# Two attentions of a fused model step: one DVE pass for mask and row maximum, and a product of two tensors on GpSimd

## The reference, cut to what matters

```python
logits = jnp.einsum('bnqhgd,bnkhd->bnhgqk', qb, kw) * (dh ** -0.5)   # dh = 64: 0.125
qi = jnp.arange(WINDOW)[:, None]; kj = jnp.arange(2 * WINDOW)[None, :]
band = (kj > qi) & (kj <= qi + WINDOW)
...
# softmax over the masked logits and one sink logit per head; the sink has no value row
```

## Time and profile before

| | |
|---|---|
| median of 3 runs | 4006.71 us (4005.89 to 4007.29) |
| time of the profiled execution | 4001.18 us |
| its span | 3999.4 us |
| PE, DVE, ACT, POOL busy | 98%, 50%, 17%, 34% |
| banded attention, first scores to first matmul of the next stage | 941.45 to 1017.20 us |
| MLA attention, the same | 2121.80 to 2214.34 us |

### The profile page before, as it was taken

One profiled execution on the slowest core, in us unless ns is written; L12 is line 12 of the kernel. 1 busy time (PEld: TensorE's weight loads), 2 busy tenths in 40 slices (PEclk: granted clock), 3 DMA queues, 4 the chain that ended last, 5 costly groups with the idle time before them and its releaser, 6 DMA issues. The chain is left out here.

```text
span 3999.4 us, 45877 instructions
## 1 busy us (share of the span) xinstructions
PE 3906.1 (98%) x18086; PEld 3000.3 (75%) x18086; DVE 2008.6 (50%) x3612; ACT 689.7 (17%) x1500; POOL 1348.7 (34%) x1145
## 2 busy tenths in 40 slices
PE   9999999997999999999999999999999989999999
PEld 4448888754588886888845688888888547858888
DVE  5547777458477763433247343243334744454333
ACT  2321110124111102100025200010001321220000
POOL 0004444204244441444306244444442051024443
PEclk9999999999999999999999999999999999999999
DMA  3115554320255352222320222222222232112222
GB/s 130 46 58 183 183 182 146 110 84 22 95 182 186 138 185 68 88 92 82 98 69 11 73 86 85 90 79 86 93 82 79 74 120 60 33 60 91 89 79 80
DMA packets 134454, 387.36 MB, mean 97 GB/s; under 512 B 39040, under 2 KB 47360, under 8 KB 124512
## 3 DMA queue, kind: packets, MB, share of 16 engines
q1 hardware_dynamic: 116912, 301.03, 22.9%
q10 hardware_dynamic: 16272, 79.90, 5.3%
q0 software_dynamic: 1056, 3.49, 0.3%
HBM read 375.26 MB, written 8.39 MB: 96 GB/s over the span
## 5 line engine op out<-in xcount | busy, mean ns | idle before, releaser
L980 PE MATMUL bank<-normed,weight_ring 128*128 128x256 f32 (+2 forms) x3632 | 997.6, 433 | 4.8 <-ACT normed L1934 1.6
L980 PEld LDWEIGHTS bank<-normed,weight_ring 128*128 128x128 f32 (+1 forms) x3632 | 670.3, 188 | 298.6 <-issue 222.3
L980 PE MATMUL bank<-area_b,weight_ring 128*128 128x256 f32 (+3 forms) x2192 | 573.4, 434 | 6.8 <-issue 2.8
L980 PEld LDWEIGHTS bank<-area_b,weight_ring 128*128 128x128 f32 (+2 forms) x2192 | 388.0, 184 | 157.6 <-issue 110.2
L876 POOL TENSOR_TENSOR area_d<-weight_ring 128x512 f32<-128x512 f32 (+1 forms) x106 | 134.3, 1267 | 929.5 <-PE bank L980 838.5
L980 PE MATMUL bank<-area_b 128*128 128x256 f32 (+2 forms) x1656 | 363.8, 376 | 13.3 <-DVE area_b L3247 10.7
L980 PE MATMUL bank<-area_a,weight_ring 128*128 128x256 f32 (+2 forms) x1424 | 371.6, 414 | 2.3 <-DMA weight_ring<-in_weights_dram 2.0
L876 POOL TENSOR_TENSOR area_b<-weight_ring 128x512 f32<-128x512 f32 (+1 forms) x102 | 130.0, 1274 | 714.3 <-PE bank L980 627.3
L980 PE MATMUL bank<-area_b,area_d 128*128 128x256 f32 x1560 | 356.2, 380 | 5.6 <-issue 5.2
L980 PEld LDWEIGHTS bank<-area_b 128*128 128x128 f32 (+1 forms) x1656 | 299.2, 191 | 70.8 <-issue 14.6
L980 PEld LDWEIGHTS bank<-area_b,area_d 128*128 128x128 f32 x1560 | 296.6, 190 | 47.8 <-issue 6.0
(11 more groups left out here) (361 smaller groups left out, 4928.3 us busy)
## 6 DMA issues: line engine op xcount, KB each, us to landing
weight_ring<-in_weights_dram SPq DMA_DIRECT2D x429, 512.0 KB, 4.6
area_b<-in_weights_dram ACTq DMA_DIRECT2D x48, 1024.0 KB, 5.0
weight_ring<-in_weights_dram SPq DMA_DIRECT2D x27, 1024.0 KB, 4.8
area_b<-in_weights_dram ACTq DMA_DIRECT2D x48, 512.0 KB, 6.2
weight_ring<-in_weights_dram SPq DMA_DIRECT2D x43, 384.0 KB, 4.3
weight_ring<-in_weights_dram SPq DMA_DIRECT2D x29, 256.0 KB, 3.9
weight_ring<-in_weights_dram SPq DMA_DIRECT2D x38, 128.0 KB, 4.1
low_scratch<-area_d ACTq DMA_DIRECT2D x16, 256.0 KB, 2.0
```

The lines of the kernel that those rows point to most:

```text
L980: i = pe.matmul(out, lhsT, rhs, start=start, stop=stop)
```

## The change

Three edits:

1. In the banded attention, each half's mask pass over 128x512 and maximum pass over 128x512 become two fused operations over 128x256, one a head: (scores + band) x 0.125 into `at_probs`, with the running maximum, begun at the sink, written to the column of that head. The operation with the sinks (L3005) falls away, and the waits of DVE for itself between the passes too. The mask is now scaled as well.
2. In MLA, the masking of the last 128 columns and the maximum become one fused operation over all (n + 1) x 128 columns, in place in PSUM. It adds a mask tile of 512 columns, 384 zeros and the causal 128, built once in front of the loop by a memset and a copy in a free part of `area_d`.
3. In both, POOL's multiplication by a per-partition scalar becomes a product of two tensors, the second of them the same [128, 1] column broadcast over the row.

```diff
+        MLA_MASK = D[:, 4, :]
...
-                    i = po.tensor_scalar(w, w, at_columns("one", v // 2)[:, 2 * (v % 2) + e:2 * (v % 2) + e + 1], None, ALU.mult)
+                    one = at_columns("one", v // 2)[:, 2 * (v % 2) + e:2 * (v % 2) + e + 1]
+                    i = po.tensor_tensor(w, w, one.to_broadcast([P, 256 - lo]), ALU.mult)
...
-                po.tensor_scalar(w, w, mla_columns("one", v // 2)[:, v % 2:v % 2 + 1], None, ALU.mult)\
+                one = mla_columns("one", v // 2)[:, v % 2:v % 2 + 1]
+                po.tensor_tensor(w, w, one.to_broadcast([P, (v // 2 % NB + 1) * P]), ALU.mult)\
                     .then_inc(S("mla_probs"), 1)
...
-                        took(stt(p, scores, 0.125, band, ALU.mult, ALU.add), m)
-                        done(dve, m)
-                        own(dve.tensor_reduce(most[:, 2 * half:2 * half + 2], p, AX, ALU.max))
+                        band = C[:, CAT["band"] + lo:CAT["band"] + 256]
+                        for e in range(2):
+                            i = dve.tensor_tensor_reduce(
+                                at_probs(u)[:, 256 * e + lo:256 * e + 256], pbank(m)[:, 256 * e + lo:256 * e + 256], band, 0.125,
+                                vec("at_sinks", 4 * g + 2 * e + half), ALU.add, ALU.max, most[:, 2 * half + e:2 * half + e + 1])
+                        took(i, m)
+                    for u in (2 * w, 2 * w + 1):
+                        done(dve, at_scores(u))
...
-                    own(tt(most, most, sinks, ALU.max))
...
+            own(dve.memset(MLA_MASK[:, 0:3 * P], 0.0))
+            own(dve.tensor_copy(MLA_MASK[:, 3 * P:T], const("causal")))
...
-                        own_keys = scores[:, n * P:(n + 1) * P]
                         dve.wait_ge(S("mla_scored"), u + 1)
-                        own(tt(own_keys, own_keys, const("causal"), ALU.add))
-                        i = dve.tensor_reduce(most[:, half:half + 1], scores, AX, ALU.max)
-                        own(i)
+                        i = dve.tensor_tensor_reduce(scores, scores, MLA_MASK[:, (3 - n) * P:T], 1.0, -3.0e38, ALU.add, ALU.max,
+                                                     most[:, half:half + 1])
+                    own(i)
```

More of the change, by code:

```diff
@@ L2997, in _ @@
                             sfull(dve, at_small("turned", u - 8))
-                        p, scores = (x.rearrange("p (e k) -> p e k", e=2)[:, :, lo:256] for x in (at_probs(u), pbank(m)[:, :]))
-                        band = C[:, CAT["band"] + lo:CAT["band"] + 256].unsqueeze(1).to_broadcast([P, 2, 256 - lo])
-                        took(stt(p, scores, 0.125, band, ALU.mult, ALU.add), m)
-                        done(dve, m)
-                        own(dve.tensor_reduce(most[:, 2 * half:2 * half + 2], p, AX, ALU.max))
+                        band = C[:, CAT["band"] + lo:CAT["band"] + 256]
[6 more added lines that the diff above has]
+                        done(dve, at_scores(u))
                     sinks = V[:, VAT["at_sinks"] + 4 * g:VAT["at_sinks"] + 4 * g + 4, 0].rearrange("p (e h) -> p h e", h=2)
                     most, less = (x.rearrange("p (h e) -> p h e", h=2) for x in (most, at_columns("sink", w)))
-                    own(tt(most, most, sinks, ALU.max))
                     own(tt(less, sinks, most, ALU.subtract))
```

## The result

| | us |
|---|---|
| forecast | 3992.0, range 3986 to 4004 |
| changed kernel, median of 4 runs | 3978.68 (3976.68 to 3980.68) |
| kernel before, beside it | 4007.0 (4005.89 to 4007.93) |
| ratio | 0.993, 95% interval 0.9914 to 0.9945 |
| profiled execution: span, time | 3976.1, 3977.93 |

The change makes the kernel 28.3 us faster. Measured once more later (run e12_changed_again), the changed kernel took 3979.37 us (3974.15 to 3980.02, 5 runs), ratio 0.9929 [0.9917, 0.9942].

What follows compares the result with a forecast made beforehand. PE, busy 98% of the span, bounds the kernel, but DVE is fullest in the settled banded attention. 12.1 us there and 2.7 us in MLA make 14.8 us off 4006.71, so 3992 us, range 3986 to 4004.

Steps and rivals of the forecast that it cites:

- The fused operation, 0.51 us: Banded attention, DVE: each of four fused operations over 128x256 takes 0.51 us, making DVE's step 3.51 us.
- What is late next: PE with 3.36 us and a hand-over of about 0.1: Banded attention, settled steps: PE nearly level with DVE, step falls from 4.52 to 3.57 us, 9.5 us won over ten.
- There PE, not DVE, will be next; I count 1.0: Banded attention, first six steps: PE's clock is between its levels, so 1.0 us of a possible 4 us is won.
- POOL in the banded attention: Banded attention: a division as a product of two tensors takes 0.69 us at 256 columns, 2.8 us a step.
- if it stayed at 3.67 us it would cost 0.1 us a step: Banded attention: what POOL's old division would cost against the forecast step of 3.57 us, 0.1 us a step.
- The end, 1.6 forecast: End of the banded attention: POOL's last eight divisions end some 1.6 us earlier.
- MLA's start, 1.0 us: First steps of MLA: DVE's shorter masking and maximum, less the mask's memset and copy, win 1.0 us.
- hidden by PE at 72.45 of 73 us; I count 0.5: MLA's settled part: PE hides the savings of DVE and POOL, so 0.5 us is won.
- the price of 0.1 us a step: MLA's settled part: if PE's cover is thinner, 0.1 us in each of 28 steps would be 3 us.
- MLA's end, 1.2 us: End of MLA: POOL's last four divisions fall from 5.54 to 4.6 us, DVE's last pair by 0.3; 1.2 us won.
- Rivals 1 and 2: Fused operation at scan's rate, 0.75 us, about 4003.7 us, chance 0.19; or with long start, about 4039 us, chance 0.07.
- 3 (1.13 us and more a division): Both attentions: POOL's product with a broadcast operand is dear, 1.49 us a piece; about 4050 us, chance 0.04.
- Rival 4: Banded attention: DVE and PE hold each other up, step 4.0 us, 3997 us; within the forecast's chance of 0.70.

Runs made afterwards that it cites:

- e12_changed_again: The changed kernel itself, unaltered, measured once more as the yardstick; 3979.37 us, ratio 0.9929 to the kernel before.
- e16: Changed kernel, but in the banded attention DVE waits for each fused operation to end before starting the next; 3987.57 us, ratio 0.9951.
- e7: Changed kernel, but with the old mask, maximum and sinks operations in the banded attention, reordered with one DVE self-wait at the end; 3989.47 us, ratio 0.9955.
- e2: Kernel before, with only POOL's product of two tensors in both attentions, DVE as before; 3999.48 us, ratio 0.9981.
- e10: Changed kernel, with negated scores and minima so both negations go, and MLA's mask built ahead of the value copies; 3976.15 us, ratio 0.9923.
- e13: Changed kernel, but PE does four of the eight transposes twice in each banded step; 3982.61 us, ratio 0.994.
- e8: Changed kernel, with two more small self-waiting DVE operations in each banded step; 3983.3 us, ratio 0.9943.
- e4: Kernel before, with the banded attention's DVE and POOL edits, MLA as before; 3985.79 us, ratio 0.9947.
- e1: Kernel before, with only the banded attention's fused operations, POOL and MLA as before; 3993.85 us, ratio 0.9968.
- e6: Kernel before, with only MLA's fused operation, POOL's old division and the banded attention as before; 4003.84 us, ratio 0.9988.
- e5: Kernel before, with both MLA edits, DVE and POOL, the banded attention as before; 3996.48 us, ratio 0.9974.
- e11: The version of e10 run again beside the changed kernel; 3976.1 us, ratio 0.9925.

## Why the prediction was right in sign and half in size

**The fused operation, 0.51 us: failed.** This is the main term. The prediction took the duration of a like pass (0.42 us) and added 0.09 us for the column. Alone, the operation does take 0.48 us, and waited for it takes 0.53 (e16). But in the change nothing waits between the four, and then they start 0.405 us apart, less than even the lower bound of 0.42. With the four at 4 x 0.405 us and 0.19 us to L3012, DVE's step is 1.81 + 1.45 = 3.26 us, where 3.51 was forecast. The rule "duration plus column" counts an end that the next start overlaps. Part of that was the removed self-waits, which the prediction named but did not price by themselves: e7 shows 0.385 of the step's 1.26 us to be theirs, the other 0.875 us the fusing with L3005. The other way round, fusing first (e2 to e16) and then taking out the waits (e16 to the changed kernel), the shares are the same, 0.877 and 0.384. A row of the kernel before would have warned me; the timeline has four copies of a bank with no wait between them,

```profile
939.68 1.41 DVE L2980 COPY area_a<-bank 128x256 f32<-128x256 f32 x4
```

each 412 ns by itself and four of them in 1.41 us: 0.33 us from start to start.

**"What is late next: PE with 3.36 us and a hand-over of about 0.1": failed.** The 3.36 us were the step less PE's named waits, so they held 0.26 us of shorter ones. PE needs 3.10 us (the trace of e10, and e13 less its four transposes), and in the changed kernel DVE alone sets the step (e8). There is no hand-over on top either: the step is DVE's 3.25 us. That floor also kept the range too high: its lower end, a pass at 0.42 us, was cut off at PE's 3.45 us. Both errors together are the 3.1 us of the settled steps.

**"There PE, not DVE, will be next; I count 1.0" for the first six steps: failed.** They gave 4.6 us, the largest miss of all. In 946 to 954 us after, at a granted clock of 0.63 on average, PE is busy 5.67 of 8 us and DVE 6.83. The averages of 0.64 and 0.63 are no level of their own: the clock was 1.00 and then 0.50, the level of 1.2 GHz, from 944.2 to 954.4 us before and from 948.0 to 954.8 us after. The slower clock made PE's work longer but cost little, since PE had that much room: e4, with the same banded code, had the low clock for 3.4 us in place of 6.8 and took 13.98 us for the six steps, 0.23 less. The edit of DVE alone (e1, with 10.2 us at the low clock as before) brought 3.7 us, 18.79 to 15.11.

**POOL in the banded attention: right, and undervalued.** 0.69 us was forecast, 0.61 measured. The sentence "if it stayed at 3.67 us it would cost 0.1 us a step" is right against 3.57, but DVE went under it, and then the edit is worth 0.30 us a step on average (e1 against e4), and 0.36 us where POOL sets the step (3.61 us). The end, 1.6 forecast, is 2.1 us: POOL's last four now take 2.32 us, and PE and DVE follow them closely.

```profile
995.72 2.32 POOL L902 TENSOR_TENSOR area_d<-area_d,small_columns 128x256 f32<-128x256 f32 x4 [0.49 <-DVE small_columns L2989]
...
1002.00 1.53 PE L984 MATMUL bank<-area_b,weight_ring 128*128 128x512 f32 x3 [1.31 <-DVE area_b L3023]
```

**MLA's start, 1.0 us: right.** The mask's memset and copy stand ahead of the first fused operation (start and length):

```profile
2107.81 0.38 DVE L3154 MEMSET area_d<- 128x384 f32 x1
2108.23 0.23 DVE L3155 COPY area_d<-constant_matrices 128x128 f32<-128x128 f32 x1
2108.54 0.30 DVE L3163 CUSTOM_DVE_ANT_0 bank<-bank,area_d 128x128 f32<-128x128 f32 x1
```

0.73 us pass from the memset to the fused operation, most of it in the time in which DVE idled before.

**MLA's settled part, "hidden by PE at 72.45 of 73 us; I count 0.5": failed, by the way that the prediction itself had named.** 2.8 us came, close to the 3 us written there for a thinner cover. PE's busy share reads 99% in both kernels (72.45 and 72.23 of 73), yet a settled round of four steps, by the starts of its transposes, fell from 10.60 to 10.28 us, and the first round from 11.08 to 10.28. Six rounds by 0.32 us and the first by 0.80 make the 2.8 us (e6 alone: 10.28 and 10.61; e2 alone: 10.36 and 10.80). The modelled ends seem to fill the gaps: the eight transposes of one step, in the traces of before and of after, start and length,

```profile
2156.00 1.28 PE L1604 MATMUL bank<-constant_matrices,area_d 128*128 128x128 f32 x8
```

```profile
2150.15 1.04 PE L1608 MATMUL bank<-constant_matrices,area_d 128*128 128x128 f32 x8
```

are the same work, 0.24 us shorter, with no wait shown in either; that is 0.24 of the 0.32 us of each round. The prediction's sentence "hidden by PE" took a busy share for a bound; the price of 0.1 us a step that it wrote beside it was right.

**MLA's end, 1.2 us: mis-sized, and half of it is the clock.** 3.9 us came. Before, PE's granted clock stood at 0.50, the level of 1.2 GHz, from 2208 to 2212 us, and its last 28 output matmuls took 3.26 us; after, the clock is 1.00 over the end, and they take 1.85.

```profile
2208.00:2212.00 4.00, 3.57 (x23) 2.76 (x22) 0.29 (x1) 1.19 (x2) 1.56 (x2) 0.50 0.00 0
```

```profile
2186.00:2192.00 6.00, 5.23 (x56) 3.77 (x58) 1.23 (x5) 3.88 (x10) 3.64 (x4) 1.00 0.01 3
```

e4, whose MLA is that of before but at a clock of 1.00 over its end, needs 8.92 us where before needs 10.77. That puts 1.85 us on the clock and 10.77 - 1.85 - 6.86 = 2.06 us on the edits. Ahead of the fall PE waited 0.72 and 0.67 us for POOL; after, its waits there are 0.42 us and shorter. Whether the change keeps the clock up, or it merely fell otherwise in these executions, the runs do not settle: with the old division in MLA it was low over the end in two traces (before, e1) and high in two (e4, e6), and with the quick one it was high in all ten (after, e2, e5, e7, e8, e10, e11, e12, e13, e16).

**The rivals.** Rivals 1 and 2 (0.75 us and more a pass) and 3 (1.13 us and more a division) are out by the rows above. Rival 4 (a step of 4.0 us) is out at 3.26. The case that was missing lies on the good side: a fused pass under 0.42 us from start to start, with a PE that can follow it.

## What to carry to other kernels

Price an operation in an in-order queue by the distance of starts, not by its duration (0.405 us against 0.48 here): look in the trace for a group of like operations with no wait between them, and for one with waits, and use the row that fits the new code. A wait of DVE for itself cost 0.128 us here, behind a pass of 512 columns as behind a fused one of 256, so such waits are a term of their own, and taking them out needs no new operation: it gave 0.385 of the 1.26 us that the step lost. And an engine's need is not the step less its named waits: what is left (3.36 us here) still holds waits too short to be named (the need was 3.10), so a floor made of it should not cut off the range. And an average over steps can hide a change of bound: e13's 3.328 us was seven steps at 3.25 and three near 3.54, so list the steps before you explain their mean.

## What the runs showed of the hardware that was not expected

- A small DVE operation can be held by POOL. MLA's L3166, two columns, took 429 ns on average after (321 before, L3159). Of the 32, 14 start while a division of POOL runs; 13 of these last 0.55 to 1.03 us and end within 0.03 us of POOL's operation, and all others take 0.17 us. The timeline after, with POOL beside it:

```profile
2167.66 2.04 POOL L919 TENSOR_TENSOR area_d<-area_d,small_columns 128x512 f32<-128x512 f32 x2 [0.60 <-DVE small_columns L3169]
...
2168.69 1.02 DVE L3166 TENSOR_SCALAR small_columns<-small_columns 128x2 f32<-128x2 f32 x1
```

  POOL's second product ends at 2169.70 and the small operation at 2169.71. At 170 ns each the 32 would take 5.4 us; they took 13.7. The fused passes and reciprocals beside it are not held. The Trainium skill (SBUF — State Buffer, "Who interferes with whom") describes one port pair that both engines share and that the loser of it waits for until the other's instruction ends, with tensor_scalar among the operations that can take it; these two rows agree. It cost nothing here: e10 has the operation no more, and MLA's settled part is the same (71.36 and 71.38 us).
- The read of the fused operation's result (83 ns in the banded attention, 142 ns in MLA) runs beside the next fused operation: both start at 984.12 above. Whether it is free is not shown: the fused operations start 0.405 us apart, the plain copies of the same width (L2980) 0.33.
